# Two heads' scores and values side by side, and the delta rule's scaled tiles made by ScalarE, in a network of two hybrid blocks

## The reference

```python
# mq, mk, mv, rq, rk, rv, gq, gk, gv, the gates and their biases: slices of one projection of the normed input
h_m = _mlstm(_heads(mq, 4), _heads(mk, 4), _heads(mv, 4), i_pre, f_pre)
y_m = _head_rmsnorm(h_m, m_out_norm) * sigmoid(mo)
h_r = _retention(_rope(_heads(rq, 4)), _rope(_heads(rk, 4)), _heads(rv, 4))
y_r = _head_rmsnorm(h_r, r_out_norm) * silu(rg)
qkv = silu(_causal_dwconv(concatenate([gq, gk, gv]), g_conv))
h_g = _gated_delta(_l2norm(_heads(cq, 4)), _l2norm(_heads(ck, 4)), _heads(cv, 4), log_alpha, beta)
y_g = _head_rmsnorm(h_g, g_out_norm) * silu(gz)
out = concatenate([y_m, y_r, y_g]) @ w_out
```

## Time and profile before

| | |
|---|---|
| time, median of 3 runs | 3358.9 us (3358.81 to 3363.27) |
| profiled execution | 3359.39 us, of it 3357.5 us from first to last instruction |
| mean granted TensorE clock | 0.992 |
| busy | TensorE 3289.8, VectorE 1725.5, ScalarE 1271.2 us |
| the two attention stages | about 423 to 598 and 1521 to 1696 us |
| the two delta rule stages | about 598 to 717 and 1696 to 1813 us |

### The profile page before, as it was taken

One profiled execution on the slowest core, in us unless ns is written; L12 is line 12 of the kernel. 1 busy time (PEld: TensorE's weight loads), 2 busy tenths in 40 slices (PEclk: granted clock), 3 DMA queues, 4 the chain that ended last, 5 costly groups with the idle time before them and its releaser, 6 DMA issues.

```text
span 3357.5 us, 38789 instructions
## 1 busy us (share of the span) xinstructions
PE 3289.8 (98%) x15294; PEld 2688.4 (80%) x15294; DVE 1725.5 (51%) x2424; ACT 1271.2 (38%) x1870; POOL 30.5 (1%) x62
## 2 busy tenths in 40 slices
PE   8999999999999999999999999999999999999998
PEld 7888876788888888887668888877888888888887
DVE  4443455765443444345575544455556577454433
ACT  4222334443222322233444332335454467332321
POOL 0000000000000000000000000000000000000000
PEclk9999999999999999999999999999999999999999
DMA  4233321113233232322211322321211233333231
GB/s 150 96 98 92 104 75 59 38 57 104 97 95 97 96 99 93 99 92 82 65 42 42 111 96 94 96 87 57 69 57 61 84 93 96 105 99 98 97 93 65
DMA packets 107396, 288.05 MB, mean 86 GB/s; under 512 B 22912, under 2 KB 34176, under 8 KB 107216
## 3 DMA queue, kind: packets, MB, share of 16 engines
q1 hardware_dynamic: 91696, 278.70, 26.1%
q10 hardware_dynamic: 14208, 2.63, 0.4%
q0 software_dynamic: 1312, 4.25, 0.4%
HBM read 282.64 MB, written 2.88 MB: 85 GB/s over the span
## 4 chain that ended last, share of the span: by engine, by line
PE 89%; DVE 6%; ACT 3%; issue 1%; ACTq 1%; DMA 1%; DVEq 0%; SPq 0%
PE ps L785 27%; PE ps L787 26%; PE ps L786 26%; PE ps L794 2%; DVE mf L2150 1%; DVE wl L1964 1%; PE ps L1101 1%; PE ps L1257 1%; PE ps L1096 1%; ACT wh L1370 1%; PE ps L1239 1%; ACT L1361 1%; PE ps L799 1%; PE ps L1253 0%; ACTq L1662 0%
## 5 line engine op out<-in xcount | busy, mean ns | idle before, releaser
L1370 ACT ACTIVATE wh<-raw 128x1024 fp32r<-128x1024 f32 (+3 forms) x581 | 567.3, 977 | 1680.3 <-PE ps L787 1647.4
L785 PE MATMUL ps<-hnh,wh 128*128 128x512 f32 x2712 | 1080.6, 398 | 2.9 <-DVE hnl L1979 2.0
L787 PE MATMUL ps<-hnh,wl 128*128 128x512 f32 x2712 | 1060.8, 391 | 0.0
L786 PE MATMUL ps<-hnl,wh 128*128 128x512 f32 x2712 | 1060.1, 391 | 0.0
L1964 DVE TENSOR_TENSOR wl<-raw,wh 128x1024 fp32r<-128x1024 f32 (+3 forms) x581 | 652.1, 1123 | 591.3 <-ACT wh L1370 588.1
L785 PEld LDWEIGHTS ps<-hnh,wh 128*128 128x128 f32 x2712 | 512.2, 189 | 123.9 <-issue 19.6
L787 PEld LDWEIGHTS ps<-hnh,wl 128*128 128x128 f32 x2712 | 511.4, 189 | 108.6
L786 PEld LDWEIGHTS ps<-hnl,wh 128*128 128x128 f32 x2712 | 512.5, 189 | 106.7 <-issue 3.4
L785 PE MATMUL ps<-mr,wh 128*128 128x512 f32 x1300 | 509.2, 392 | 2.8 <-DVE mr L2626 2.0
L787 PE MATMUL ps<-mr,wl 128*128 128x512 f32 x1300 | 506.1, 389 | 0.0
L786 PE MATMUL ps<-mr,wh 128*128 128x512 f32 x1300 | 505.9, 389 | 0.0
(11 more groups left out here) (293 smaller groups left out, 2407.4 us busy)
## 6 DMA issues: line engine op xcount, KB each, us to landing
raw<-in_w_in SPq DMA_DIRECT2D x140, 512.0 KB, 3.5
raw<-in_ffn_w_gate SPq DMA_DIRECT2D x88, 512.0 KB, 3.5
raw<-in_ffn_w_up SPq DMA_DIRECT2D x88, 512.0 KB, 3.5
raw<-in_ffn_w_down SPq DMA_DIRECT2D x64, 512.0 KB, 3.5
raw<-in_w_ffn_in SPq DMA_DIRECT2D x44, 512.0 KB, 3.5
raw<-in_ffn_w_down SPq DMA_DIRECT2D x32, 384.0 KB, 3.0
raw<-in_w_out SPq DMA_DIRECT2D x32, 256.0 KB, 2.6
raw<-in_w_out_ssm SPq DMA_DIRECT2D x32, 256.0 KB, 2.6
```

Source lines behind the costliest of these rows:

```text
L785: self.e.matmul(out, ah, bh, start=start, stop=False, skip_group_check=shared)
L786: self.e.matmul(out, ah, bl, start=False, stop=False, skip_group_check=shared)
L787: m = self.e.matmul(out, al, bh, start=False, stop=stop, skip_group_check=shared)
L1370: self.e.activation(k.spl[u % NSPL][0][:, 0:n], k.raw[u % NRAW][:, 0:n], ACT.Copy).then_inc(k.w_hi, 1)
```

## The change

Attention: the two heads of a pair are taken together. Spread, arguments and exponential of each come in steps 0 to 4 of 16, the scores of both heads alternate (`scores`, widths 512, 384 and 128 in one step, 256 five steps later), each head in its own PSUM bank. The weights of the second head have their own slots (M_D and R_D), the weighing comes in four steps, and the values follow two to five steps behind it. The retention's values of the two heads alternate, each with 64 columns to its own half of the partitions, and are taken out by one instruction of ScalarE. All four retention tables have slots of their own; GpSimd loads the last two behind the mLSTM's last values, ahead of its two memsets. The attention has 70 steps at a pace of 1.05; slots of the queries, keys and values of the delta rule are ordered by kind. Delta rule: vb, kd and kb are each made by four ScalarE instructions of 128x128 with a column as scale; TensorE waits for ScalarE's vb ahead of spread rq, and for its kb ahead of y4. The diff, cut:

```diff
-PACE_ROWS, PACE_ATT, PACE_BOTH, PACE_DELTA = 1.1, 0.98, 2.0, 1.3
+PACE_ROWS, PACE_ATT, PACE_BOTH, PACE_DELTA = 1.1, 1.05, 2.0, 1.3
...
-M_Q, M_K, M_V, M_D, M_NG, M_EM = 32, 34, 36, 40, 43, 44
-R_Q, R_K, R_V, R_D, R_TAB = 20, 22, 24, 28, (43, 44)
-D_SQ, D_R, D_BLK, D_PART = (36, 37, 38, 39, 34, 35, 16, 19), 31, 42, 100
+M_Q, M_K, M_V, M_D, M_NG, M_EM = 32, 34, 36, (40, 17), 43, 44
+R_Q, R_K, R_V, R_D, R_TAB = 20, 22, 24, (28, 17), (43, 44, 38, 39)
+D_SQ, D_R, D_BLK, D_PART = (36, 37, 38, 39, 34, 35, 16, 42), 31, 42, 100
...
+SCORE_AT = ((((6, 0), (2, 0)), ((7, 0), (3, 0)), ((6, 0), (2, 0)), ((7, 384), (3, 384))))
...
-ATT_STEPS, AT_ROPE, AT_RET = 65, 34, 40
+ATT_STEPS, AT_ROPE, AT_RET, PER_PAIR, PER_RET = 70, 34, 42, 16, 9
+OF_PAIR = "s0 t0 s1 t1 s3 t3 s2 t2"
...
     def attention(self, l, y):
         for t in range(ATT_STEPS):
-            h, s = divmod(t, 8)
...
+            for p in range(2):
+                self.mlstm(l, p, t - PER_PAIR * p)
+            for p in range(2):
+                self.mlstm_pair(l, p, t - PER_PAIR * (p + 1))
             self.rope(l, t - AT_ROPE)
-            if t >= AT_RET:
...
+            for p in range(2):
+                self.retention(l, p, t - AT_RET - PER_RET * p)
+                self.retention_pair(l, p, t - AT_RET - PER_RET * p)
             yield
...
         self.wait_ge(*act(2))
         self.turn(b, four(V_), 128, k.c("ident"), P.up(l, "vT"))
         yield
-        self.wait_ge(*V.at(l, "vb"))
+        self.wait_ge(*A.at(l, "vb"))
         self.spread(k.slot(D_T2, dt=R), h, B_HEAD[h], P.up(l, "rq"))
         yield
         self.wait_ge(*V.at(l, "q"))
@@ -1052,6 +1057,8 @@
         self.wait_ge(k.blk_set, 256 * (l + 1))
         for i in range(4, 7):
             self.wait_ge(*V.at(l, f"am{i}"))
+            if i == 4:
+                self.wait_ge(*A.at(l, "kb"))
             if i > 4:
...
-    def score(self, q, kk, h, jt, up):
...
+    def scores(self, q, kk, p, jt, ups):
+
+        k, w = self.k, T - 128 * jt
+        for s in range(2):
+            (bank, at), pr = SCORE_AT[jt][s], slice(64 * s, 64 * s + 64)
+            m = self.e.matmul(k.ps[bank][:, at:at + w], k.slot(kk + p)[pr, 128 * jt:128 * jt + 128], k.slot(q + p)[pr, 128 * jt:T],
+                              start=True, stop=True, skip_group_check=True)
+            if ups:
+                m.then_inc(*ups[s]())
+
+    def mlstm(self, l, p, s):
+        k, n = self.k, 2 * l + p
         P, A, V = k.mh_p, k.mh_a, k.mh_v
-        if h >= 4:
-            return
-        n = 4 * l + h
-        if s == 0:
+        up = lambda *names: [lambda name=name: P.up(n, name) for name in names]
+        if s in (0, 2):
             self.wait_ge(k.row_v, 5 * l + 2)
             self.wait_ge(*k.rows_v.at(l, "acol"))
-            if h:
...
+            if s:
+                self.wait_ge(*V.at(n, "dm0"))
+            elif p:
+                self.wait_ge(*V.at(n - 1, "dm1"))
+            self.spread(k.slot(M_NG, dt=R), 2 * p + s // 2, B_PAIR, P.up(n, f"sp{s // 2}"))
+        if s == 4:
+            if p:
+                self.wait_ge(*V.at(n - 1, "t2"))
             self.wait_ge(k.took, self.qk_took[2 * l])
+            self.scores(M_Q, M_K, p, 0, up("s0", "t0"))
+            self.scores(M_Q, M_K, p, 1, None)
+            self.scores(M_Q, M_K, p, 3, up("s3", "t3"))
+        if s == 9:
+            self.wait_ge(*V.at(n, "t0"))
+            self.scores(M_Q, M_K, p, 2, up("s2", "t2"))
+        if s in (13, 16):
+            i = (s - 13) // 3
+            self.wait_ge(k.took, self.v_took[2 * l])
+            if i or p:
+                self.wait_ge(*(A.at(n, "abs0") if i else A.at(n - 1, "abs1")))
+            self.wait_ge(*V.at(n, ("s2", "t2")[i]))
             for jt in range(4):
-                self.score(M_Q, M_K, h, jt, P.up(n, f"s{jt}"))
...
+                h = 2 * p + i
+                m = self.e.matmul(k.ps[B_ATT][:, 128 * jt:T], k.slot(M_V + jt)[:, 128 * h:128 * h + 128],
+                                  k.slot(M_D[i], 3)[:, OFF[jt]:OFF[jt] + T - 128 * jt], start=jt == 0, stop=jt == 3)
+            m.then_inc(*P.up(n, f"v{i}"))
...
     def mlstm_pair(self, l, p, s):
         k, n = self.k, 2 * l + p
-        if s == 2:
+        if s == 5:
             self.wait_ge(k.row_v, 5 * l + 1)
-            self.wait_ge(*k.mh_v.at(4 * l + min(2 * p + 2, 3), "dm"))
+            self.wait_ge(*k.mh_v.at(2 * l + 1, "dm1"))
+            if p:
+                self.wait_ge(*k.mp_v.at(n - 1, "sum"))
             self.e.matmul(k.ps[B_PAIR][:, :], k.selr[0:64, 32 + 128 * p:160 + 128 * p], k.slot(M_EM, dt=R)[0:64, :],
                           start=True, stop=True).then_inc(*k.mp_p.up(n, "pair"))
-        if s == 5:
+        if s == 9:
             self.wait_ge(*k.mp_a.at(n, "sq"))
             self.e.matmul(k.ps[B_PAIR][:, :], k.c("bd64"), k.slot(M_Y + p)[:, :], start=True, stop=True).then_inc(*k.mp_p.up(n, "nm"))
...
-    def retention(self, l, h, s):
-        k = self.k
+    def retention(self, l, p, s):
+        k, n = self.k, 2 * l + p
         P, A, V = k.rh_p, k.rh_a, k.rh_v
-        if h >= 4:
-            return
-        n = 4 * l + h
+        up = lambda *names: [lambda name=name: k.rh_s.up(n, name) for name in names]
         if s == 0:
-            self.wait_ge(*(V.at(n - 1, "w3") if h else k.rope_v.at(4 * l + 3, "x")))
+            self.wait_ge(*(V.at(n - 1, "t2") if p else k.rope_v.at(4 * l + 3, "x")))
+            self.scores(R_Q, R_K, p, 0, up("s0", "t0"))
+            self.scores(R_Q, R_K, p, 1, None)
+            self.scores(R_Q, R_K, p, 3, up("s3", "t3"))
+        if s == 5:
+            self.wait_ge(*V.at(n, "t0"))
+            self.scores(R_Q, R_K, p, 2, up("s2", "t2"))
+        if s == 10:
+            self.wait_ge(k.took, self.v_took[2 * l + 1])
+            self.wait_ge(*(A.at(n - 1, "num") if p else k.mh_a.at(2 * l + 1, "abs1")))
+            self.wait_ge(*V.at(n, "t2"))
             for jt in range(4):
-                self.score(R_Q, R_K, h, jt, P.up(n, f"s{jt}"))
...
+                for i in range(2):
+                    at = 128 * (2 * p + i) + 64 * i
+                    m = self.e.matmul(k.ps[B_ATT][64 * i:64 * i + 64, 128 * jt:T], k.slot(R_V + jt)[:, at:at + 64],
+                                      k.slot(R_D[i], 3)[:, OFF[jt]:OFF[jt] + T - 128 * jt], start=jt == 0, stop=jt == 3,
+                                      skip_group_check=True)
             m.then_inc(*P.up(n, "v"))
...
-        if c < 24 and c % 12 >= 10:
+        if c < 24 and c % 12 == 8:
             self.wait_ge(*k.dr_p.at(c // 12, "ss1"))
...
         self.wait_ge(*k.mp_v.at(2 * l + 1, "on"))
+        self.wait_ge(*k.rh_v.at(2 * l + 1, "t2"))
...
-        for _ in range(6):
-            yield
+        yield
+        yield
+
+        def by_columns(to, columns, up):
+            for t, x, w in zip(four(to), four(b), range(4)):
+                m = e.activation(t, x, ACT.Copy, scale=columns[:, w:w + 1])
+            m.then_inc(*up)
+
+        self.wait_ge(*P.at(l, "vT"))
+        by_columns(k.slot(of_head(2, h)), of_kind(k.d_cols, 3, h), A.up(l, "vb"))
+        yield
+        yield
+        yield
+        self.wait_ge(*P.at(l, "kT"))
+        by_columns(k.slot(D_KB[h]), sd[:, 0:4], A.up(l, "kd"))
+        by_columns(K, of_kind(k.d_cols, 1, h), A.up(l, "kb"))
+        yield
...
-        self.wait_ge(*P.at(l, "vT"))
-        e.tensor_tensor(blk(vb), blk(b), wide(of_kind(k.d_cols, 3, h)), ALU.mult).then_inc(*V.up(l, "vb"))
...
-        self.wait_ge(*P.at(l, "kT"))
-        e.tensor_tensor(blk(kb), blk(b), wide(sd[:, 0:4]), ALU.mult).then_inc(*V.up(l, "kd"))
-        e.tensor_tensor(blk(K), blk(b), wide(of_kind(k.d_cols, 1, h)), ALU.mult).then_inc(*V.up(l, "kb"))
         self.wait_ge(*V.at(l, "qg"))
         e.tensor_tensor(blk(am), blk(a), mask(4), ALU.mult).then_inc(*V.up(l, "am4"))
...
     def weigh(self, P, V, n, d, jt, by):
-        k = self.k
...
+
+        k, w = self.k, T - 128 * jt
+        for i, name in enumerate("st"):
+            bank, at = SCORE_AT[jt][i]
+            self.wait_ge(*P.at(n, f"{name}{3 if jt == 1 else jt}"))
+            self.e.tensor_tensor(k.slot(d[i], 3)[:, OFF[jt]:OFF[jt] + w], k.ps[bank][:, at:at + w], by[i][:, 0:w],
+                                 ALU.mult).then_inc(*V.up(n, f"{name}{jt}"))
+
+    def mlstm(self, l, p, s):
+        k, e, n = self.k, self.e, 2 * l + p
...
-        if s in (4, 5):
-            self.wait_ge(*A.at(n, "w"))
-            for jt in (2 * s - 8, 2 * s - 7):
-                self.weigh(P, V, n, M_D, jt, d[:, OFF[jt]:])
+            m.then_inc(*V.up(n, f"dm{i}"))
+        if s in (6, 7, 8, 11):
+            jt = {6: 0, 7: 1, 8: 3, 11: 2}[s]
+            self.wait_ge(*A.at(n, "w1"))
+            self.weigh(P, V, n, M_D, jt, [k.slot(d, 3)[:, OFF[jt]:] for d in M_D])
...
+        if s in (2, 3, 4, 7):
+            jt = {2: 0, 3: 1, 4: 3, 7: 2}[s]
+            self.wait_ge(k.loaded[f"ret{2 * p}"], 16 * (l + 1))
+            self.wait_ge(k.loaded[f"ret{2 * p + 1}"], 16 * (l + 1))
```

(15 more changed lines are left out.)

## The result

The changed kernel takes 3368.23 us (median), the kernel before 3360.3 us in the runs beside it: ratio 1.0024, interval 1.0018 to 1.0031, 7.9 us slower. The forecast was 3364.5, 5.1 us slower than the profiled run of before. The profiled run of after has a span of 3364.3 us.

What follows compares the result with a forecast made beforehand. TensorE's own instruction stream plus its stalls was taken as the bound (busy 98%). Work -14.4, attention stalls +2.5, ScalarE's scaling +13.0 and clock +4 summed to +5.1 us on 3359.39: forecast 3364.5, range 3345 to 3380.

Steps and rivals of the forecast that it cites:

- TensorE's work, at full clock: Both mixers: paired scores save 6.0 (retention) and 3.1 (mLSTM), retention values 5.3, together -14.4 us.
- stalls outside the last chain: Both mixers: attention stalls +2.5, waits for vb at rq +8.7, less waiting at the transposes of k -1.8.
- chain, with the wait ahead of the first y4: Delta rule's end: kd and kb queued behind 16 DMA issues, +0.6 at the first y4 and +5.5 after it.
- clock outside both: TensorE's clock halves after new stalls: two short stretches of 1.7 us and a little, +4 us (0 to +11).
- Scores: Attention: two heads' scores on different row halves overlap in part, 2.56 and 1.05 us blocks, saving 6.0 us in the retention.
- Retention values: Retention: two heads' values on different column halves overlap, with entry cost, saving 5.3 us (ends +6.9 and -1.6).
- Attention stalls: Attention, both mixers: longer waits at the burst's second spread and mLSTM norm, shorter values' waits, +2.5 us (0 to +5).
- Relief by VectorE: Delta rule: VectorE's old stall of TensorE at the transposes of k shrinks by 0.9 us per mixer, -1.8.
- ScalarE's queue: Delta rule: vb, kd and kb wait behind DMA issues and landing in ScalarE's in-order queue, +13.0 us in all.
- Rival B: ScalarE's queue costs next to nothing while the pairing gives all: 3347 us, chance 0.27.
- C: On the array, column halves run in turn, 3371.5 us (0.10), or no float32 passes of two heads overlap, 3385 (0.03).
- D: Each stall at rq and y4 over some 3 us draws a long half-clock stretch, +9.6 us, 3374; chance 0.15.

Runs made afterwards that it cites:

- due_back: The changed kernel with the paces' remainder behind the second mixer set back to 0.8, the value of before: 3362.65 us, ratio 1.0009.
- before_due: The kernel before with the paces' remainder behind the second mixer set to 0.2, the changed kernel's value: 3368.43 us, ratio 1.0026.
- again: The changed kernel run once more, nothing altered: 3367.83 us.
- halves_in_turn: The pairing alone (remainder 0.8, scaling on VectorE) with the retention's values loops exchanged, one head's four matmuls after the other's: 3350.88 us.
- pair_due: The changed kernel with the remainder set to 0.8 and the scaling of vb, kd and kb given back to VectorE: 3344.31 us, ratio 0.9956.
- gpsimd_vector: The changed kernel with remainder 0.8, block transfers' issues moved to GpSimd and all scaling back on VectorE: 3339.93 us.
- issues_on_gpsimd: The changed kernel with remainder 0.8, scaling still on ScalarE, block transfers' 27 issues a mixer moved from ScalarE to GpSimd: 3340.73 us, ratio 0.9943.

## Why the prediction was right, and where it was not

The time fell inside the range and on the forecast side, but partly by luck: inside the mixers the gain was larger than forecast and the stalls were too, and the two errors cancelled for the most part. On top of that 5.2 us came from a stage that the forecast took as unchanged; the range had room for them. The change itself, due_back against before, is 3.1 us by the medians (0 to 6.0), so the forecast 5.1 is not excluded for it. By the steps of the sum, for the two mixers, first from the traces of before and after, then from the means of all traces with the same mixers (before and before_due; after, again and due_back):

| Term | forecast | measured | means |
|---|---|---|---|
| TensorE's work, at full clock | -14.4 | -20.2 | -20.2 |
| stalls outside the last chain | +9.4 | +13.7 | +12.2 |
| chain, with the wait ahead of the first y4 | +6.1 | +4.7 | +4.4 |
| clock outside both | +4 | +2.7 | +5.3 |
| mixers in all | +5.1 | +1.5 | +2.3 |
| beyond the mixers | 0 | +5.2 | |

Work is the sum of all blocks between projections, each at the smallest value that a block of the same matmuls has in any trace: 145.7 us before, 125.5 after. Clock is what blocks and the starts of projections take above that: 29.9 and 32.6. Stalls are 22.9 and 36.6, the chain 111.8 and 116.5; 0.6 us stays unassigned. The forecast's 0.6 for the landing stands in the chain's row, since its wait is counted there. The last row is again against due_back, by their medians.

- **Scores.** The step that failed here is "only a head's second pass and the other head's first overlap". 2.13 us is 4 passes of 512 columns and 0.40, 0.83 is one and 0.40: the passes of both heads overlap wholly, two for two, as their starts 0.007 us apart show. A retention pair costs 2.96 where it cost 5.12: 2.16 x 4 = 8.7 us saved, not 6.0. The 0.40 of entry was right, and it is paid by the split-off block too. With 7.2 us from the retention's values (next point) this leaves 4.3 of the 20.2 for the mLSTM, by difference, where 3.1 stood.
- **Retention values.** 2.51 in place of 4.32: 1.81 x 4 = 7.2 us, not 5.3. The upper bound of the prediction, 6.9, was too low, for the same reason. halves_in_turn shows that it is the alternation of the halves.
  The Trainium skill ("TensorE: Matmul & The Clock Gate", Part 3: Packing small matmuls) has column tiles run concurrently, which had given 2.2 us and 8.7. The trace agrees on the concurrency, 2.51 is five passes of 0.433 and 0.35, and decides on the gain: the block pays that entry on top.
- **Attention stalls.** The burst's second spread in the second mixer waits 4.4 (forecast 4.4), the mLSTM norm 3.8 and 2.5 (1.9 over 2.1 is 4.0; 0.6 over 2.1 is 2.7), and the values' own waits shrank to nothing and 0.2. Two were not foreseen: the retention norm waits 3.2 in the first mixer, where 1.0 stood, because ScalarE's square (L1751, 543.8) is queued behind a SiLU that waits for VectorE's taps, and the first spread of an odd head waits 1.0. So 2.5 became about 5.9 us.
- **Relief by VectorE.** The prediction had VectorE's old stall of TensorE at the transposes of k shrink by 0.9 in each mixer, since less is queued there. It did not: 2.3 and 2.0 us before, 2.0 and 2.5 after, so that -1.8 became +0.2. With the 5.9 above and 7.1 at rq (8.7 forecast) this makes 13.2 of the 13.7.
- **ScalarE's queue.** rq 3.5 and 3.7 us (forecast 3.8, with the heads behind it 4.3), the first y4 and the chain +4.7 (6.1, or 5.9 without a slip of rounding: 9.0 - 5.46 and 9.0 - 7.22 make 5.3 and not 5.5). So each is off by a quarter or less. The scaling's whole price, 13.0 and most of the 4 of clock, is 17 by forecast and 18.3 by due_back against pair_due. Some 8 of the 21.4 us in the two traces, over a third, is put down to the lower clock, which I had kept as a separate small term. Rival B (the queue is hidden) falls: pair_due shows what it would have given, 3344 for the forecast of 3347.
- **The instruction's own price.** I took the Trainium skill's rule ("ScalarE: Activation LUTs", Rules for kernel authors), multiplications to VectorE, as one of bare prices and put it aside. gpsimd_vector against issues_on_gpsimd gives 0.8 us for VectorE, the way of the rule, but inside the scatter.
- **Outside the mixers.** The prediction took all stages but the mixers as unchanged. That was wrong: the paces' remainder moved, and with it the order of ScalarE's and VectorE's work in the recurrent layers. The variable stands in the code of before, and its value behind each stage can be worked out from the paces and the number of steps, as I had done for the mixers. With the remainder held at 0.8 the answer would have been "no change that can be told": due_back is 1.0009.
- **Rivals C and D.** C falls with 2.13 and 2.51. D was right in kind: in or right behind the stalls at rq and at the first y4 of both mixers the granted clock reads 0.50 in four stretches of the long kind (622.7 to 629.5, 656.8 to 663.6, 1721.8 to 1728.6, 1755.9 to 1766.1). Its condition, a stall of over 3 us, did not decide it: the waits at the two first y4 were 1.47 and 2.05. And its size, 9.6 on top of 4, didn't come, +2.7 to +5.3 outside the chain.

## What to carry to other kernels

Before a step is given to an engine with room, look at what stands ahead of it in that engine's in-order queue at that moment; issues of transfers and waits for their landing count in full, and the instruction's own price may count for little (0.8 us in all here). Where a queue is the trouble, move the issues (here to an idle engine, 21.9 us) and not the step. A scheduler with a carried remainder spreads a local edit over everything behind it: fix the remainder before you compare, or you measure two changes.

## What the runs showed of the hardware

Float32 matmuls on two row halves, issued alternately, run fully side by side, both passes (6 matmuls in 2.13 us, 4 passes of 512 columns and 0.40). Two column halves do too when they alternate (2.51 us against 4.07 one half after the other). An issue of a 16 KB transfer takes 0.56 us on GpSimd and 0.48 to 0.62 on ScalarE in these traces; the 16 of a mixer take 8.93 and 7.96 us. And TensorE came back from the waits of over 3 us at rq at the lower level of its clock, and the scaling, whose stalls and chain cost 6.5 and 7.1 us, cost some 8 more in matmuls issued more slowly.
